# Cross-attention scores of a two-block decoder: one float32 product becomes three terms of rounded and remaining parts

## The chip, the cores and the metric

One core of one Trainium2 chip runs the whole program in one launch. The metric is the device time of one execution in microseconds (us); the median of three runs of the kernel before is 2508.31 us (2506.42 to 2509.89). The engines are named as in the profile: PE (TensorE, matmuls; PEld is its weight load), DVE (VectorE), ACT (ScalarE), POOL (GpSimd) and SP (SyncE, which here only issues DMAs).

## What is computed

Two stacks of layers on 512 tokens of width 1024, in float32. The change lies in the cross-attention of the second block, which reads 256 memory tokens with 4 heads of width 256:

```python
def memory_cross_attention(x, mem, g_x, g_m, wq, wk, wv, wo):
    b, s, _ = x.shape
    h = rms_norm(x, g_x)
    m = rms_norm(mem, g_m)
    q = (h @ wq).reshape(b, s, XATTN_HEADS, XATTN_HEAD_DIM)
    k = (m @ wk).reshape(b, m.shape[1], XATTN_HEADS, XATTN_HEAD_DIM)
    v = (m @ wv).reshape(b, m.shape[1], XATTN_HEADS, XATTN_HEAD_DIM)
    sc = jnp.einsum("bshd,bmhd->bhsm", q, k).astype(jnp.float32) * (XATTN_HEAD_DIM ** -0.5)
    p = jax.nn.softmax(sc, axis=-1)
    o = jnp.einsum("bhsm,bmhd->bshd", p.astype(v.dtype), v).reshape(b, s, D_MODEL)
    return o @ wo
```

Everything else (retention layers, sparse attention, gated mixers, feed-forward parts, norms) is the same in both kernels.

## The kernel before

**Tiling.** Activations lie feature by feature in SBUF: a tile of 512 tokens (`T`) for each of the 8 blocks (`KB`) of 128 features. A product with a weight matrix is cut into units; unit `f` makes 128 output features for all tokens and ends in the bank `unit_ps[f % 2]`. It is 24 matmuls of 128x512: 8 blocks of the inner dimension times three terms, since nearly every product is made of float32r operands, a rounded part (`wh`, `ah`, `ch`) and what remains of the value (`wl`, `al`, `cl`): `wh*xh + wh*xl + wl*xh`.

**Who does what for a unit's weights.** SP loads 512 KB into `raw[u % 2]` once POOL is done with the unit two before it. ACT rounds it into `wh` (one instruction of 128x1024, in `ahead2(XQ + f)`: it waits for the end of unit `f` and for the landing of the weights of unit `f + 4`). POOL makes `wl = raw - wh` in two instructions of 128x512 and counts `w_lo` (L472).

**The stretch of the query projection, units XQ to XQ+7.** It follows the output projection of the mixers (`OUT`) and a norm: DVE sums the squares, PE averages them (`ssq`), ACT takes the root (L530) and DVE the reciprocal `rstd` (L1286). Each engine has its own hand-written order:

- PE: unit 0, `ssq`, unit 1, unit 2, `x_scores(0)`, unit 3, `x_turns(0)` (transposes of the weights of head 0), unit 4, `x_values(0)`, `x_scores(1)`, unit 5, `x_turns(1)`, unit 6, `x_values(1)`, `x_scores(2)`, unit 7, `x_turns(2)`, `x_scores(3)`, then the first units of the output projection `XO` with the rest of heads 2 and 3 between them. Head `h` reads the query units `2h` and `2h + 1`. A unit waits for its bank: unit `f` for the eviction of unit `f - 2`.
- DVE, for `f` from 0 to 7: waits for unit `f`, evicts it (`mult`, `xq_t[f] = unit_ps * rstd`, L1276 in the profile, line 1707 in the loop), and then, for `f` of 0 and 1, makes the remaining part `vl` of the memory's values (L1711); for odd `f` from 3 the remaining part of the transposed weights (L1696); for even `f` from 2 the softmax of head `(f - 2) / 2` (L1684 maximum, L1686, L1689 and a product on L1276), ahead of it from 4 on the remaining part of a head's result (L1703).
- ACT: the root, two copies of 128x1024 that round the memory's values (`vh`, L835), and then for each `f` the weights of unit `f + 4` (L495), for odd `f` the rounded transposed weights (L850), for even `f` the rounded result (L855) and the exponentials (L842).

`x_scores(h)` multiplies float32 operands directly, for 4 blocks of 128 tokens and 2 blocks of the head's width: the queries `xq_t` (in `d1`) are the stationary operand, the memory keys `mem_k` (in `b_f32`) the moving one of 256 columns:

```python
for c in range(NC):
    for b in range(2):
        last = pe.matmul(aux[:, 2 * (h % 2) + c // 2, (c % 2) * MEM:(c % 2 + 1) * MEM], xq_t[2 * h + b][:, c * P:(c + 1) * P],
                         mem_k[:, (2 * h + b) * MEM:(2 * h + b + 1) * MEM], start=(b == 0), stop=(b == 1))
last.then_inc(xs_mm, 1)
```

`go()` makes a DVE instruction wait for the one before it, and `did(...)` counts it. In the profile `xq_t` and the softmax's `x_p` both read as `d`, `vh` and `vl` as `bl`, `xth` and `xtl` as `bh`, and `mem_k` and `mem_v` as `b_f`.

Of the kernel before, what the change touches and what calls it, by code (L numbers as in the profile page):

```python
# [27 lines left out]
F32 = mybir.dt.float32  # L28
F32R = mybir.dt.float32r
I32 = mybir.dt.int32  # L30
BF16 = mybir.dt.bfloat16
ALU = mybir.AluOpType
ACT = mybir.ActivationFunctionType
AX = mybir.AxisListType.X

P = 128
T = 512
D = 1024
KB = D // P
# [27 lines left out]
MEM = 256  # L67
# [20 lines left out]
XQ = OUT + KB  # L88
# [45 lines left out]
def layer_stack_kernel(nc, d, out):  # L134

    ctx = ExitStack()
    with ctx:
        def sb(name, shape, dt=F32):
            return ctx.enter_context(nc.sbuf_tensor(name, shape, dt))

        def sem(name):
            return ctx.enter_context(nc.semaphore(name))
# [12 lines left out]
        bh, bl = sb("bh", [P, KB * T], F32R), sb("bl", [P, KB * T], F32R)  # L155
        with nc.sbuf_tensor("c_f32", [P, 2 * KB * T], F32) as c_f32:
            cf = c_f32
        ch, cl = sb("ch", [P, KB * T], F32R), sb("cl", [P, KB * T], F32R)
        d1, d2 = sb("d1", [P, KB * T]), sb("d2", [P, KB * T])

        with (nc.sbuf_tensor("decay_t", [P, HEADS * T], F32) as decay_t, nc.sbuf_tensor("cos_t", [P, T], F32) as cos_t,
# [20 lines left out]
        rstd = sb("rstd", [P, T])  # L182
        tmp = [sb(f"tmp{i}", [P, T]) for i in range(2)]
# [59 lines left out]
        mem_k = bf[:, 4 * T:8 * T]  # L243
        mem_v = bf[:, 12 * T:16 * T].rearrange("p (c v) -> p c v", c=2)
# [5 lines left out]
        p_first = d1[:, 2 * T:6 * T].rearrange("p (r k) -> p r k", r=REP)  # L250
        part_x = [d1[:, (4 + i) * T:(5 + i) * T] for i in range(2)]
        ffn_t = [d1[:, i * T:(i + 1) * T] for i in range(4)]
        xq_t = [d1[:, f * T:(f + 1) * T] for f in range(KB)]
        vh, vl = (bl[:, at:at + 4 * T].rearrange("p (c v) -> p c v", c=2) for at in (0, 4 * T))
        x_p = d2[:, 2 * T:4 * T].rearrange("p (c m) -> p c m", c=NC)
        xth, xtl = (bh[:, at:at + 2 * T].rearrange("p (m q) -> p m q", m=2) for at in (0, 2 * T))
# [1 line left out]
        unit_ps = [ctx.enter_context(nc.psum_tensor(f"unit_ps{i}", [P, T], F32)) for i in range(2)]  # L258
        aux = ctx.enter_context(nc.psum_tensor("aux", [P, 4, T], F32))
# [25 lines left out]
        w_hi, w_lo, mm, evac = sem("w_hi"), sem("w_lo"), sem("mm"), sem("evac")  # L285
# [27 lines left out]
        src2 = sem("src2")  # L313
        mean_out = sem("mean_out")
        w_att, p_act = sem("w_att"), sem("p_act")
        v_hi, v_lo, xt_lo = sem("v_hi"), sem("v_lo"), sem("xt_lo")
        xs_mm, xs_shift, x_exp, xp_ready, xt_mm, xt_copy, xo_mm = (sem(n) for n in (
            "xs_mm", "xs_shift", "x_exp", "xp_ready", "xt_mm", "xt_copy", "xo_mm"))
# [7 lines left out]
        def half_blk(t, k, half):  # L326

            return t[:, k * T + half * T // 2:k * T + (half + 1) * T // 2]
# [157 lines left out]
        def _(act):  # L486
# [5 lines left out]
            def split_w(u, j):  # L492

                act.wait_ge(raw_in[j % 2], 16 * 1 + (u - j % 2) * 8)
                act.activation(wh[j][:], raw[j % 2][:], ACT.Copy).then_inc(w_hi, 1)  # L495
# [32 lines left out]
            def sqrt_ms(n, dst=rstd[:], src=stat_ps, bias=eps[:, 0:1]):  # L528
                act.wait_ge(ssq_mm, n)
                act.activation(dst, src, ACT.Sqrt, bias=bias).then_inc(std_done, 1)  # L530
# [114 lines left out]
            def ahead2(u):  # L645

                act.wait_ge(mm, u + 1)
                if u + 4 < U_END:
                    split_w(u + 4, u % 4)
# [37 lines left out]
            for i in range(2):  # L687
                for g in range(2):
                    out_g = 1 - g if i else g
                    lanes = slice(out_g * HD, out_g * HD + HD)  # L690
# [141 lines left out]
            norm_units2(OUT, 2, ch, sq_out)  # L832
            sqrt_ms(LAYERS * 2 + 3)
            for m in range(2):
                act.activation(vh[:, m], mem_v[:, m], ACT.Copy).then_inc(v_hi, 1)  # L835


            def x_exps(h):
                act.wait_ge(xs_shift, h + 1)
                s_x = aux[:, 2 * (h % 2):2 * (h % 2) + 2].rearrange("p b (c m) -> p (b c) m", m=MEM)  # L840
                for c in range(NC):
                    act.activation(x_p[:, c], s_x[:, c], ACT.Exp, scale=DV ** -0.5,  # L842
                                   bias=row[:, 0, c:c + 1], accum_out=row[:, 1, c:c + 1]).then_inc(x_exp, 1)

            def x_turned(h):
                for m in range(2):
                    act.wait_ge(xt_mm, 2 * h + m + 1)
                    if h:
                        act.wait_ge(xo_mm, 2 * h)
                    act.activation(xth[:, m], o_ps[m], ACT.Copy).then_inc(xt_copy, 1)  # L850

            def x_hi(h):
                for b in range(2):
                    act.wait_ge(xo_mm, 2 * h + b + 1)
                    act.activation(blk(ah, 2 * h + b), aux[:, 2 * (h % 2) + b], ACT.Copy).then_inc(in_hi, 1)  # L855

            for f in range(KB):
                ahead2(XQ + f)
                if f % 2:
                    if f >= 3:  # L860
                        x_turned((f - 3) // 2)
                elif f >= 2:
                    if f >= 4:
                        x_hi((f - 4) // 2)
                    x_exps((f - 2) // 2)
# [59 lines left out]
        def _(dve):  # L925
# [337 lines left out]
            last = [(dve_step, step[0])]  # L1263

            def go():

                dve.wait_ge(*last[0])

            def did(ins, s=dve_step):
                count[id(s)] = count.get(id(s), 0) + 1  # L1270
                ins.then_inc(s, 1)
                last[0] = (s, count[id(s)])

            def mult(dst, a, b, s=dve_step):
                go()
                did(dve.tensor_tensor(dst, a, b, ALU.mult), s)  # L1276
# [115 lines left out]
            for k in range(KB):  # L1392
                dve.wait_ge(mem_hi, k // 2 * 2 + 2)
                lanes = slice(k * MEM, (k + 1) * MEM)
# [297 lines left out]
            def x_turned_lo(h):  # L1692
                for m in range(2):
                    dve.wait_ge(xt_copy, 2 * h + m + 1)
                    go()
                    did(dve.tensor_tensor(xtl[:, m], o_ps[m], xth[:, m].bitcast(F32), ALU.subtract), xt_lo)  # L1696

            def x_lo(h):
                for b in range(2):
                    k = 2 * h + b  # L1700
                    dve.wait_ge(in_hi, IL + k + 1)
                    go()
                    did(dve.tensor_tensor(blk(al, k), aux[:, 2 * (h % 2) + b], blk(ah, k).bitcast(F32), ALU.subtract), in_lo)  # L1703

            for f in range(KB):
                dve.wait_ge(mm, XQ + f + 1)
                mult(xq_t[f], unit_ps[(XQ + f) % 2][:], rstd[:], evac)
                if f < 2:
                    dve.wait_ge(v_hi, f + 1)
                    go()  # L1710
                    did(dve.tensor_tensor(vl[:, f], mem_v[:, f], vh[:, f].bitcast(F32), ALU.subtract), v_lo)  # L1711
                elif f % 2:
                    x_turned_lo((f - 3) // 2)
                else:
                    if f >= 4:
                        x_lo((f - 4) // 2)
                    x_softmax((f - 2) // 2)
# [107 lines left out]
        def _(pe):  # L1825
# [192 lines left out]
            for n in range(CMP_BLOCK):  # L2018
                for i in range(2):
                    for g in range(2):  # L2020
                        lanes = slice(g * HD, g * HD + HD)
                        out_g = 1 - g if i else g
                        last = pe.matmul(aux[out_g * HD:out_g * HD + HD, 2 * i + g, 0:N_CMP], cmp_w1[i][lanes, n], cmp_win[i][lanes, n],
                                         start=(n == 0), stop=(n == CMP_BLOCK - 1))
# [4 lines left out]
            for g in range(2):  # L2029
                lanes = slice(g * HD, g * HD + HD)  # L2030
                pe.matmul(o_ps[0][lanes, 0:N_CMP], cmp_w2[0][lanes], cmp_hid[0][lanes], start=True, stop=True).then_inc(cmp_mm, 1)
            for g in range(2):
                lanes = slice((1 - g) * HD, (1 - g) * HD + HD)
# [4 lines left out]
            for c in range(NC):  # L2038
                for i in range(2):
                    last = pe.transpose(aux[:, c // 2, (c % 2) * DV + i * P:(c % 2) * DV + (i + 1) * P], y_gm[i][:, c * P:(c + 1) * P], ident[:])  # L2040
# [21 lines left out]
            for k in range(KB):  # L2062
                for c in range(2):
                    col = (k % 2) * MEM + c * P
                    last = pe.transpose(aux[:, k // 2, col:col + P], mem_raw[:, c, k * P:(k + 1) * P], ident[:])
# [115 lines left out]
            for i in range(2):  # L2181
                for c in range(NC):
                    for half in range(2):
                        g = 2 * i + half
                        last = pe.matmul(o_ps[i][half * HD:half * HD + HD, c * P:(c + 1) * P], v_ln[:, c, g * HD:(g + 1) * HD], gm_wt[:, g * P:(g + 1) * P],
                                         start=True, stop=True)
# [57 lines left out]
            for at in range(4, KB):  # L2244
                pe.wait_ge(in_lo, IL + at + 1)
                for f in range(2):
                    last = out_part(f, PART_ORDER[at], at)
                    if at == KB - 1:
                        last.then_inc(mm, 1)
            for f in range(2, 4):  # L2250
                for at in range(4, KB):
                    last = out_part(f, PART_ORDER[at], at)
# [3 lines left out]
            IL += 2 * KB  # L2256

            def x_scores(h):
                pe.wait_ge(evac, XQ + 2 * h + 1 + 3)
                if h >= 2:  # L2260
                    pe.wait_ge(in_lo, IL + 2 * (h - 2) + 2)
                for c in range(NC):
                    for b in range(2):
                        last = pe.matmul(aux[:, 2 * (h % 2) + c // 2, (c % 2) * MEM:(c % 2 + 1) * MEM], xq_t[2 * h + b][:, c * P:(c + 1) * P],  # L2264
                                         mem_k[:, (2 * h + b) * MEM:(2 * h + b + 1) * MEM], start=(b == 0), stop=(b == 1))
                last.then_inc(xs_mm, 1)

            def x_turns(h):
# [49 lines left out]
            for k in (6, 7):  # L2318
                pe.wait_ge(in_lo, IL + k + 1)
                for f in range(2):  # L2320
                    last = xo_part(f, (k,))
# [21 lines left out]
            for n, (u, f, half) in enumerate(LAST_PARTS):  # L2343
# [3 lines left out]
                for k in range(n_k):  # L2347
                    for q, (w, v) in enumerate(((wh, ah), (wh, al), (wl, ah))):
                        last = pe.matmul(unit_ps[u % 2][:, 0:T // 2], w[(DNG[2] + f) % 4][:, k], half_blk(v, k, half),  # L2349
                                         start=(k == 0 and q == 0), stop=(k == n_k - 1 and q == 2))  # L2350
# [91 lines left out]
```

## Time and profile before

| | |
|---|---|
| median of 3 runs | 2508.31 us (2506.42 to 2509.89) |
| the profiled execution, its own time | 2508.62 us |
| its span, first to last instruction | 2506.8 us |
| PE busy | 2488.3 us, 99% |
| PEld, DVE, ACT, POOL busy | 82%, 49%, 37%, 50% |
| the chain that ended last: PE, DVE, ACT | 95%, 4%, 1% |
| the score matmuls (L2264) | 64 records, 14.6 us busy |
| granted clock of PE | 0.997 of full speed (2.4 GHz) |

A span is what the trace covers; the 1.8 us between it and the execution's own time lie around it. A float32 matmul leaves two records, so the 64 records of L2264 are 32 matmuls. Where one engine is busy throughout, what counts is what it executes and where it stands still; idle time of the others costs nothing until PE waits for them.

### The profile page before, as it was taken

To read this page: it belongs to the slowest core of one execution; us is meant where nothing else is said; L and a number is where in the kernel's file an instruction comes from. 1 tells how busy PE (TensorE), PEld (TensorE's weight loads), DVE (VectorE), ACT (ScalarE), POOL (GpSimd) and SP (SyncE) were. 2 spreads that over 40 slices of the span, in tenths; PEclk is the share of its full clock that TensorE was granted. 3 is DMA by queue.
4 is the path that set the end of the run, shared out by engine and by line. 5 is a ranking of instruction groups with operands and counts; after the bars stand their busy time and mean duration, and the time that the engine had idled before them with its cause. 6 is when DMAs were issued, how large, how long until landed. Compare 5 with 4: busy or idle time off the path is not lost.

```text
span 2506.8 us, 34796 instructions
## 1 busy us (share of the span) xinstructions
PE 2488.3 (99%) x11934; PEld 2050.8 (82%) x11934; DVE 1226.6 (49%) x1436; ACT 917.4 (37%) x1322; POOL 1257.5 (50%) x879
## 2 busy tenths in 40 slices
PE   9999999999999999999999999999999999999998
PEld 8888888888888888888888888888877888888887
DVE  7444612453322542555135423227887755788364
ACT  5223423332222332334234322223457644444233
POOL 6555355655545554544455545555523443555454
PEclk9999999999999999999999999999999999999999
DMA  5332233333333333322333333337321232333332
GB/s 166 101 92 85 67 100 93 101 93 101 92 101 93 101 93 99 94 76 76 99 94 101 93 99 95 97 96 161 87 59 60 76 93 68 92 99 94 100 91 78
DMA packets 441982, 235.38 MB, mean 94 GB/s; under 512 B 16145, under 2 KB 436113, under 8 KB 441873
## 3 DMA queue, kind: packets, MB, share of 16 engines
q1 hardware_dynamic: 441440, 233.26, 32.4%
q8 instruction: 67, 1.10, 0.2%
q10 hardware_dynamic: 432, 0.67, 0.1%
q14 instruction: 43, 0.34, 0.0%
HBM read 231.81 MB, written 2.10 MB: 93 GB/s over the span
## 4 chain that ended last, share of the span: by engine, by line
PE 95%; DVE 4%; ACT 1%; issue 0%; DMA 0%; DVEq 0%; ACTq 0%
PE unit_ps L1847 62%; PE unit_ps L1992 13%; PE unit_ps L1978 7%; PE aux L1884 2%; PE unit_ps L1884 1%; PE o_banks L1884 1%; DVE c_f L1313 1%; PE aux L2220 1%; PE aux L2114 1%; PE unit_ps L2082 1%; PE unit_ps L2154 1%; PE o_banks L1925 1%; PE aux L2264 1%; PE aux L2052 0%; PE aux L2285 0%; PE unit_ps L2349 0%
## 5 line engine op out<-in xcount | busy, mean ns | idle before, releaser
L472 POOL TENSOR_TENSOR wl<-raw,wh 128x512 fp32r<-128x512 f32 x862 | 1251.1, 1472 | 1229.2 <-ACT wh L543 819.6
L543 ACT ACTIVATE wh<-raw 128x1024 fp32r<-128x1024 f32 x304 | 322.6, 1061 | 1023.7 <-PE unit_ps L1847 965.9
L1847 PE MATMUL unit_ps<-ah,wh 128*128 128x512 f32 x1280 | 503.1, 393 | 0.0
L1847 PE MATMUL unit_ps<-ah,wl 128*128 128x512 f32 x1280 | 498.6, 390 | 0.0
L1847 PE MATMUL unit_ps<-al,wh 128*128 128x512 f32 x1280 | 498.6, 390 | 0.0
L1847 PE MATMUL unit_ps<-bh,wh 128*128 128x512 f32 x768 | 300.1, 391 | 0.0
L1847 PE MATMUL unit_ps<-bh,wl 128*128 128x512 f32 x768 | 299.1, 389 | 0.0
L1847 PE MATMUL unit_ps<-bl,wh 128*128 128x512 f32 x768 | 299.1, 389 | 0.0
L1847 PEld LDWEIGHTS unit_ps<-al,wh 128*128 128x128 f32 x1280 | 240.3, 188 | 51.5 <-issue 1.9
L1847 PEld LDWEIGHTS unit_ps<-ah,wh 128*128 128x128 f32 x1280 | 240.3, 188 | 51.0 <-issue 1.9
L1847 PEld LDWEIGHTS unit_ps<-ah,wl 128*128 128x128 f32 x1280 | 240.3, 188 | 50.0
L495 ACT ACTIVATE wh<-raw 128x1024 fp32r<-128x1024 f32 x111 | 117.8, 1061 | 184.7 <-PE unit_ps L1992 111.9
L1847 PEld LDWEIGHTS unit_ps<-bh,wh 128*128 128x128 f32 x768 | 144.2, 188 | 30.8 <-issue 1.0
L1847 PEld LDWEIGHTS unit_ps<-bl,wh 128*128 128x128 f32 x768 | 144.1, 188 | 30.3 <-issue 0.5
L1847 PEld LDWEIGHTS unit_ps<-bh,wl 128*128 128x128 f32 x768 | 144.1, 188 | 30.0
L1244 DVE TENSOR_TENSOR x<-unit_ps,x 128x512 f32 x48 | 33.2, 692 | 213.5 <-PE unit_ps L1847 213.5
L1992 PE MATMUL unit_ps<-ch,wl 128*128 128x512 f32 x320 | 124.6, 389 | 0.0
L1992 PE MATMUL unit_ps<-ch,wh 128*128 128x512 f32 x320 | 124.6, 389 | 0.0
L1992 PE MATMUL unit_ps<-cl,wh 128*128 128x512 f32 x320 | 124.6, 389 | 0.0
L1234 DVE TENSOR_TENSOR tmp<-unit_ps,rstd 128x512 f32<-128x512 f32 x64 | 44.2, 691 | 134.8 <-PE unit_ps L1847 134.0
L1743 DVE SCALAR_TENSOR_TENSOR d<-tmp,vectors,d 128x511 f32<-128x511 f32 x88 | 106.0, 1205 | 1.5
L1847 PE MATMUL unit_ps<-ch,wh 128*128 128x512 f32 x256 | 99.7, 389 | 0.0
(403 smaller groups left out, 3873.3 us busy)
## 6 DMA issues: line engine op xcount, KB each, us to landing
raw<-w_in_dram SPq DMA_DIRECT2D x144, 512.0 KB, 4.0
raw<-w_up_dram SPq DMA_DIRECT2D x64, 512.0 KB, 4.0
raw<-w_down_dram SPq DMA_DIRECT2D x64, 512.0 KB, 4.1
raw<-up_dram SPq DMA_DIRECT2D x44, 512.0 KB, 3.8
raw<-w_conv_out_dram SPq DMA_DIRECT2D x16, 512.0 KB, 4.1
raw<-w_ret_out_dram SPq DMA_DIRECT2D x16, 512.0 KB, 4.1
raw<-w_o_dram SPq DMA_DIRECT2D x16, 512.0 KB, 4.1
raw<-down_dram SPq DMA_DIRECT2D x16, 512.0 KB, 3.9
```

The costliest lines, as they stand in the source:

```text
L472: last = pool.tensor_tensor(wl[j][:, half], raw[j % 2][:, half], wh[j][:, half].bitcast(F32), ALU.subtract)
L495: act.activation(wh[j][:], raw[j % 2][:], ACT.Copy).then_inc(w_hi, 1)
L543: act.activation(wh[j][:], raw[j % 2][:], ACT.Copy).then_inc(w_hi, 1)
L1234: dve.tensor_tensor(tmp[0][:], unit_ps[j % 2][:], rstd[:], ALU.mult).then_inc(evac, 1)
L1244: dve.tensor_tensor(blk(x, f), unit_ps[j % 2][:], blk(x, f), ALU.add).then_inc(evac, 1)
L1313: did(dve.scalar_tensor_tensor(out=cv_a[i], in0=src, scalar=w, in1=cv_a[i], op0=ALU.mult, op1=ALU.add))
L1743: did(dve.scalar_tensor_tensor(out=into, in0=tmp[n % 2][:, 0:T - s_], scalar=ffn_taps[:, w_, b:b + 1], in1=into, op0=ALU.mult, op1=ALU.add ...
L1847: last = pe.matmul(unit_ps[j % 2][:], w[j][:, k], v[:, k * T:(k + 1) * T], start=(k == 0 and n == 0), stop=(k == KB - 1 and n == 2))
L1884: last = pe.matmul(v_ps[group][c], v[:, col:col + P], two_k(w[j])[:, k], start=(k0 + k == 0 and w is wh and v is ah), stop=(k0 + k == KB - ...
L1925: last = pe.matmul(o_ps[b][:, n * P:(n + 1) * P], v_tok[:, n, col:col + P], p_dec[h % 2][:, n * P:(n + 1) * P], start=True, stop=(n == 0))
L1978: last = pe.matmul(dst, w[u % 4][:, k], v[:, k * n:(k + 1) * n], start=(k == 0 and q == 0), stop=(k == n_k - 1 and q == 2))
L1992: last = pe.matmul(unit_ps[u % 2][:], w[u % 4][:, k], v[:, k * T:(k + 1) * T], start=(at == 0 and q == 0), stop=(at == n_k - 1 and q == 2))
```

## The change

The scores of a head are made as `qh*kh + ql*kh + qh*kl` in float32r. The keys are split once: ACT rounds them into `kh` with two copies of 128x1024, which stand ahead of the two copies of the values, and DVE writes the remaining part `kl` over `mem_k`. A query unit no longer goes from its bank to `xq_t`: DVE evicts it to `tmp[f % 2]`, ACT rounds it into `xqh`, DVE subtracts into `xql`, and only then the unit's query is ready. `x_scores(h)` waits for `q_lo` instead of `evac`. In the profile of the new kernel `kh`, `xqh` and `xql` read as `d_f32r` and `kl` as `bh`.

```diff
+        xqh, xql = ([dr[:, at + f * T:at + (f + 1) * T] for f in range(4)] for at in (0, 12 * T))
+        kh, kl = dr[:, 4 * T:8 * T], bh[:, 4 * T:8 * T]
...
             sqrt_ms(LAYERS * 2 + 3)
             for m in range(2):
+                lanes = slice(m * D, (m + 1) * D)
+                act.activation(kh[:, lanes], mem_k[:, lanes], ACT.Copy).then_inc(k_hi, 1)
+            for m in range(2):
                 act.activation(vh[:, m], mem_v[:, m], ACT.Copy).then_inc(v_hi, 1)
...
             for f in range(KB):
                 ahead2(XQ + f)
+                act.wait_ge(evac, XQ + f + 3)
+                act.activation(xqh[f % 4], tmp[f % 2][:], ACT.Copy).then_inc(q_hi, 1)
...
             for f in range(KB):
                 dve.wait_ge(mm, XQ + f + 1)
-                mult(xq_t[f], unit_ps[(XQ + f) % 2][:], rstd[:], evac)
-                if f < 2:
-                    dve.wait_ge(v_hi, f + 1)
-                    go()
-                    did(dve.tensor_tensor(vl[:, f], mem_v[:, f], vh[:, f].bitcast(F32), ALU.subtract), v_lo)
+                mult(tmp[f % 2][:], unit_ps[(XQ + f) % 2][:], rstd[:], evac)
+                if f == 0:
+                    for m in range(2):
+                        lanes = slice(m * D, (m + 1) * D)
+                        dve.wait_ge(k_hi, m + 1)
+                        go()
+                        did(dve.tensor_tensor(kl[:, lanes], mem_k[:, lanes], kh[:, lanes].bitcast(F32), ALU.subtract), k_lo)
+                dve.wait_ge(q_hi, f + 1)
+                go()
+                did(dve.tensor_tensor(xql[f % 4], tmp[f % 2][:], xqh[f % 4].bitcast(F32), ALU.subtract), q_lo)
+                if f == 1:
+                    for m in range(2):
+                        dve.wait_ge(v_hi, m + 1)
+                        go()
+                        did(dve.tensor_tensor(vl[:, m], mem_v[:, m], vh[:, m].bitcast(F32), ALU.subtract), v_lo)
+                elif f == 0:
+                    pass
                 elif f % 2:
                     x_turned_lo((f - 3) // 2)
...
             def x_scores(h):
-                pe.wait_ge(evac, XQ + 2 * h + 1 + 3)
+                pe.wait_ge(q_lo, 2 * h + 2)
+                if h == 0:
+                    pe.wait_ge(k_lo, 2)
...
                     for b in range(2):
-                        last = pe.matmul(aux[:, 2 * (h % 2) + c // 2, (c % 2) * MEM:(c % 2 + 1) * MEM], xq_t[2 * h + b][:, c * P:(c + 1) * P],
-                                         mem_k[:, (2 * h + b) * MEM:(2 * h + b + 1) * MEM], start=(b == 0), stop=(b == 1))
+                        k = 2 * h + b
+                        lanes = slice(k * MEM, (k + 1) * MEM)
+                        for n, (q, kk) in enumerate(((xqh, kh), (xql, kh), (xqh, kl))):
+                            last = pe.matmul(aux[:, 2 * (h % 2) + c // 2, (c % 2) * MEM:(c % 2 + 1) * MEM], q[k % 4][:, c * P:(c + 1) * P], kk[:, lanes],
+                                             start=(b + n == 0), stop=(b == 1 and n == 2))
```

**How the orders move.** On DVE, from the reciprocal of the norm to the end of the softmax of head 0, the kernel before has:

```order
RECIPROCAL rstd<-rstd 128x512
TENSOR_TENSOR d<-unit_ps,rstd 128x512
TENSOR_TENSOR bl<-b_f,bl 128x1024
TENSOR_TENSOR d<-unit_ps,rstd 128x512
TENSOR_TENSOR bl<-b_f,bl 128x1024
TENSOR_TENSOR d<-unit_ps,rstd 128x512
TENSOR_REDUCE row<-aux 128x4
TENSOR_SCALAR row<-row 128x4
RECIPROCAL row<-row 128x4
TENSOR_TENSOR d<-d,row 128x1024
```

and the changed one, at the same place:

```order
RECIPROCAL rstd<-rstd 128x512
TENSOR_TENSOR tmp<-unit_ps,rstd 128x512
TENSOR_TENSOR bh<-b_f,d_f32r 128x1024 x2
TENSOR_TENSOR d_f32r<-tmp,d_f32r 128x512
TENSOR_TENSOR tmp<-unit_ps,rstd 128x512
TENSOR_TENSOR d_f32r<-tmp,d_f32r 128x512
TENSOR_TENSOR bl<-b_f,bl 128x1024 x2
TENSOR_TENSOR tmp<-unit_ps,rstd 128x512
TENSOR_TENSOR d_f32r<-tmp,d_f32r 128x512
TENSOR_REDUCE row<-aux 128x4
TENSOR_SCALAR row<-row 128x4
RECIPROCAL row<-row 128x4
```

The two subtractions of the keys stand ahead of the query of unit 0, both subtractions of the values now stand between the queries of units 1 and 2, and each eviction is followed by a subtraction of its own.

On ACT, from the root of the norm to the exponentials of head 0, before:

```order
ACTIVATE rstd<-aux,eps 128x512
ACTIVATE bl<-b_f 128x1024 x2
ACTIVATE wh<-raw 128x1024 x3
ACT_TABLE_LOAD
ACTIVATE d,row<-aux,row 128x256 x4
```

and changed:

```order
ACTIVATE rstd<-aux,eps 128x512
ACTIVATE d_f32r<-b_f 128x1024 x2
ACTIVATE bl<-b_f 128x1024 x2
ACTIVATE wh<-raw 128x1024
ACTIVATE d_f32r<-tmp 128x512
ACTIVATE wh<-raw 128x1024
ACTIVATE d_f32r<-tmp 128x512
ACTIVATE wh<-raw 128x1024
ACTIVATE d_f32r<-tmp 128x512
ACT_TABLE_LOAD
ACTIVATE d,row<-aux,row 128x256 x4
```

The rounding of a weight (`wh<-raw`) and that of a query (`d_f32r<-tmp`) now take turns, and the first weight stands behind two copies more.

## Rows read from the trace of the kernel before

**Rows 1.** The page: busy time and share of each engine.

```profile
PE 2488.3 (99%) x11934; PEld 2050.8 (82%) x11934; DVE 1226.6 (49%) x1436; ACT 917.4 (37%) x1322; POOL 1257.5 (50%) x879
```

**Rows 2.** The chain that ended last, in the query projection: start us, us, what.

```profile
2033.90 3.45 PE aux L2264 x16
2037.36 5.46 PE unit_ps L1978 x24
2042.82 0.87 PE o_banks L2274 x8
...
2078.77 0.87 PE o_banks L2274 x8
2079.64 3.63 PE aux L2264 x16
2083.27 2.75 PE unit_ps L2303 x12
2086.02 2.73 PE aux L2285 x12
```

**Rows 3.** The same view, near the end of the program.

```profile
2479.92 8.29 PE unit_ps L2349 x69
```

**Rows 4.** The timeline of DVE: start us, us, what, [idle before <-releaser].

```profile
2027.23 0.69 DVE L1276 TENSOR_TENSOR d<-unit_ps,rstd 128x512 f32<-128x512 f32 x1
2027.83 1.22 DVE L1711 TENSOR_TENSOR bl<-b_f,bl 128x1024 fp32r<-128x1024 f32 x1
2029.15 0.69 DVE L1276 TENSOR_TENSOR d<-unit_ps,rstd 128x512 f32<-128x512 f32 x1
2029.76 1.53 DVE L1711 TENSOR_TENSOR bl<-b_f,bl 128x1024 fp32r<-128x1024 f32 x1
...
2037.39 1.23 DVE L1684 TENSOR_REDUCE row<-aux 128x4 f32<-128x1024 f32 x1 [2.76 <-PE aux L2264]
...
2041.04 1.22 DVE L1276 TENSOR_TENSOR d<-d,row 128x1024 f32<-128x1024 f32 x1
```

**Rows 5.** The timeline of DVE, of units of OUT, then of POOL in single instructions.

```profile
2012.75 0.69 DVE L1667 TENSOR_TENSOR d<-d 128x512 f32<-128x512 f32 x1
...
2017.70 1.61 DVE L1667 TENSOR_TENSOR d<-d 128x512 f32<-128x512 f32 x1
...
2018.71 1.74 POOL L472 TENSOR_TENSOR wl<-raw,wh 128x512 fp32r<-128x512 f32 x1
...
2027.87 2.34 POOL L472 TENSOR_TENSOR wl<-raw,wh 128x512 fp32r<-128x512 f32 x1
...
2030.25 2.19 POOL L472 TENSOR_TENSOR wl<-raw,wh 128x512 fp32r<-128x512 f32 x1
```

**Rows 6.** The timeline of ACT.

```profile
2023.60 2.00 ACT L835 ACTIVATE bl<-b_f 128x1024 fp32r<-128x1024 f32 x2
2025.50 1.05 ACT L495 ACTIVATE wh<-raw 128x1024 fp32r<-128x1024 f32 x1
2028.50 1.06 ACT L495 ACTIVATE wh<-raw 128x1024 fp32r<-128x1024 f32 x1 [1.95 <-PE unit_ps L1978]
2034.18 1.06 ACT L495 ACTIVATE wh<-raw 128x1024 fp32r<-128x1024 f32 x1 [4.62 <-DMA raw<-wq_dram]
...
2050.54 0.60 ACT L855 ACTIVATE ah<-aux 128x512 fp32r<-128x512 f32 x1 [0.30 <-PE aux L2285]
```

**Rows 7.** Instructions that touch the tile raw, 2020 to 2050: the way from issue to landing.

```profile
DMA to landing us min/median/max: 3.7/3.8/3.9
```

**Rows 8.** The timelines behind the end of unit 7: ACT, DVE, POOL.

```profile
2078.80 1.06 ACT L495 ACTIVATE wh<-raw 128x1024 fp32r<-128x1024 f32 x1 [2.06 <-PE unit_ps L1978]
...
2078.80 0.69 DVE L1276 TENSOR_TENSOR d<-unit_ps,rstd 128x512 f32<-128x512 f32 x1 [0.59 <-PE unit_ps L1978]
2080.38 1.49 DVE L1696 TENSOR_TENSOR bh<-o_banks,bh 128x512 fp32r<-128x512 f32 x2 [0.88 <-ACT bh L850]
...
2079.94 2.50 POOL L472 TENSOR_TENSOR wl<-raw,wh 128x512 fp32r<-128x512 f32 x2 [9.10 <-ACT wh L495]
```

## Prediction of the time after the change

> **What bounds the kernel now.** I read the page's busy shares first: PE is busy 99% of the span [rows 1], every other engine half of it or less. So an edit counts by what it takes from PE's work and by the time for which it makes PE stand still. Then the chain that ended last, in the stretch of the query projection: it stays on PE without a gap, from the scores of head 0 through unit 3 to the transposes, and again from the transposes of head 2 through the scores of head 3 into the output projection [rows 2]. Nothing there is slack on PE; every wait that the change makes PE take is added in full. Last, the timelines of DVE, ACT and POOL beside it show how close each hand-over is.
>
> **Part 1: what PE executes.** The scores of a head are 16 records in 3.45 us [rows 2], 8 float32 matmuls of 431 ns. They become 8 x 3 = 24 float32r matmuls of 256 columns. The nearest rows of that form are the last units of the program, 69 matmuls in 8.29 us, 120 ns each [rows 3], with as many weight loads. 24 x 0.120 = 2.88 us, 0.57 less for a head, and for four heads **-2.3 us**. The bounds are narrow: a loss of weight-load cover would show in [rows 3] too, since each of those matmuls has its own load.
>
> The page "TensorE: Matmul & The Clock Gate" of the Trainium skill (Back-to-back issue gap) gives 262 cycles for 256 columns, 109 ns at 2.4 GHz. By it a head would be 2.6 us and the four would save 3.3 us instead of 2.3, and the sum below would be 1.0 us lower; the row says 120 ns, and I keep the row.
>
> **Part 2: what two SBUF operands cost on DVE.** The new subtractions read both operands from SBUF, and so must be priced beside POOL. Alone such an instruction is 0.69 us for 512 columns [rows 5] and 1.22 for 1024 [rows 4]. Beside POOL the two engines take turns. DVE's 1.22 us from 2027.83 to 2029.05 stretched the POOL instruction of 2027.87 to 2.34, that is to 2030.21, 1.16 us after DVE ended; DVE's next, begun at 2029.76, ended at 2031.29, 1.08 after that, and POOL's next at 2032.44, 1.15 after that [rows 4, 5]. DVE does get its turn between POOL's two halves: its instruction of 2017.70 ended at 2019.31, and POOL's second half (from 2018.71) only 1.14 later, at 2020.45 [rows 5]. An eviction, which reads a bank, kept its 0.69 us while POOL ran [rows 4]. So in contention: 512 columns 0.55 us once its turn has come, 1024 columns 1.08, a POOL half 1.15, and each waits for the other's current instruction.
>
> The Trainium skill has the rule ("SBUF — State Buffer", Who interferes with whom): a DVE instruction with two SBUF inputs and a GpSimd instruction that reads SBUF exclude each other for a whole instruction, one with a single SBUF input does not. The trace agrees. The old way out of the bank was of the harmless kind, the new `ql` is of the other; without the rule the sum below is 0.2, with it 4.4.
>
> **Part 3: the first head.** I carry the steps forward on the clock of this trace (us after 2000). Unchanged: the eviction of unit 0 starts at 27.23, unit 1 ends at 28.3, unit 2 at 33.7.
> - ACT copies the keys before the values. Two copies took 1.9 us from 23.60 to the weights at 25.50 [rows 6]; four end at 27.4. Weights 4: 27.4 to 28.45 (1.9 us later than now). Query 0 (an ACT copy of 512 columns, 0.60 [rows 6]): to 29.0. Weights 5: to 30.0.
> - DVE and POOL: `kl` first half 27.83 to 29.05; POOL 29.05 to 30.20; `kl` second half to 31.28; POOL's second half to 32.43; `ql` of unit 0 to 32.98; then POOL's first half of weights 5 to 34.13, beside it the eviction of unit 1 to 33.8 and ACT's rounding of it to 34.45. POOL's second half took its turn at 34.13, so `ql` of unit 1 waits for 35.4 and ends at 35.95. PE wants it at 33.75: **stall of 2.2 us** ahead of the scores of head 0. Scores to 38.9, unit 3 to 44.3.
> - DVE goes on with `vl` twice, 36.05 to 38.6, evicts unit 2 by 39.4 (a job that was done at 2034.6 before), ACT rounds it by 40.05. The weights of unit 6 were requested when POOL finished those of unit 4, 32.43, and land 3.8 us later [rows 7]; ACT rounds them at 36.4 to 37.5, and POOL's halves run after `vl` to 39.75 and 41.03. So `ql` of unit 2 ends at 41.6 and the softmax of head 0 begins at 41.7. It takes 4.87 us from its maximum to the end of its product (2037.39 to 2042.26, [rows 4]): 46.55. The transposes, which PE reached with 0.5 us in hand before (2042.26 against 2042.82), now wait from 44.3 to 46.6: **stall of 2.2 us**. The exponential table's load falls behind the rounding of query 2 and is hidden by the wait for the maximum.
>
> The two stalls hang together: what matters is that DVE's chain ends at 46.6, where PE without stalls would be at 33.74 + 2.88 + 5.46 = 42.1. Together **+4.5 us**. Without POOL in the way (0.69 and 1.22 each, turns not taken) the same chain gives `ql` of unit 1 at 33.3, no first stall, and an end of the softmax at 43.1: +1.0. That is the lower bound.
>
> **Part 4: heads 1 and 2.** Here I cost the change at nothing. Between the end of unit 4 or 6 and the end of the scores PE has `x_values` and the scores, 2.73 + 2.88 us; the query is rounded behind the weights 1.65 us after the unit's end and `ql` takes up to 1.35 more (both as in part 5), and the softmax begins with the scores' end as before. The cover is 2.6 us; if it were gone, each head would lose its excess at the transposes.
>
> **Part 5: the last head.** Between unit 7 and the scores of head 3 stand only transposes of 0.87 us [rows 2]. From unit 7's end (2078.78): eviction to 2079.49, weights on ACT 2078.80 to 2079.86 [rows 8], rounding of the query behind them from 2079.77 to about 2080.4. `ql` could start at 2080.43, where the remaining part of the transposed weights starts now [rows 8]. POOL has begun its first half at 2079.94 [rows 8] and holds until 2081.2; `ql` ends at 2081.8. PE is ready at 2079.65: **+2.15 us**; without POOL in the way `ql` ends at 2081.1, +1.45. The softmax of head 3 hides behind the same 5.5 us of PE work as now.
>
> **Sum.** -2.3 + 4.5 + 2.15 = **+4.4 us**. The profiled execution, 2508.62 us (span 2506.8 and 1.8 around it), becomes 2513.0; it stands 0.3 above the median of the three runs, so on the median's scale 2508.3 + 4.4 = 2512.7 us.
>
> **The rivals.**
> - *POOL is not in the way* (its halves and DVE's subtractions miss each other): -2.3 + 1.0 + 1.45 = +0.2, 2508.5 us. Against it: POOL's weights follow ACT's at once, and ACT's stand right ahead of each query. In between lies the case in which one `ql` of the first units slips ahead of a POOL half: +3.2, 2511.5 us.
> - *The stalls vanish and only the saving stays*: 2506.0 us. It would need `ql` of unit 7 within 0.87 us of the unit's end, against an eviction and a rounding of 0.69 + 0.6 alone.
> - *Clearly slower*: a POOL instruction that is already queued is let in ahead of a waiting DVE one, so that POOL keeps both halves together. The place is each `ql` behind weights just rounded: unit 7 (+1.2, a half), and units 0 and 2, whose ends set the chain of part 3 (+1.15 each). Two of the three give +6.7, 2515.0, all three 2516.2. It decides from the first of them on: +5.5 is past 0.2%. For it: a half begins the moment the other ends. Against it: the turns of [rows 5].
>
> **How the numbers follow.** 0.2% of this time, 5.0 us, is about what a measurement can tell from no change, so the line is at 2513.3. The forecast (both mechanisms as priced, 2511.8 to 2513.8) has 0.56, of which 0.09 lies over the line; POOL less in the way, 2508.5 to 2511.5, 0.20; clearly slower 0.21; the saving alone or better 0.03, of which 0.01 is under 2503.3. Faster 0.01, same 0.69, slower 0.30. The range takes the whole forecast, most of the case with less of POOL, and the slower case with two turns lost: 2509.0 to 2515.0.
>
> **What would show it.** The chain should show 24 records of the score line in 2.9 us for a head. PE should stand idle at three places: before the scores of head 0 and of head 3 with the `ql` line as releaser, and before the transposes of head 0 with the softmax's product, 2.2 us each. The subtraction lines should show 512 columns in 0.7 to 1.8 us and not 0.69 throughout. Heads 1 and 2 should show no wait. I am wrong in part 3 if POOL's rows of 2.3 us are missing, in part 1 if the 24 records take more than 3 us, and in part 4 if the transposes of head 1 or 2 wait.

## The result, and the profile after

The changed kernel takes 2513.63 us (median of 9 runs, 2512.51 to 2519.94) against 2508.78 us for the kernel before, 9 runs in the same comparison: a ratio of 1.0024, 95% interval 1.0016 to 1.0032. It is slower, by 4.9 us between the medians, or by 6.0 by the ratio. In a second comparison it was 2514.39 against 2507.48 us (1.0023, 1.0014 to 1.0032). The forecast was 2512.7 us in a range of 2509.0 to 2515.0.

The page of the profiled execution, which with 2519.94 us was the slowest of the nine, says little by itself. What answers to [rows 1]:

```profile
span 2518.2 us, 34891 instructions
...
PE 2493.8 (99%) x11966; PEld 2055.8 (82%) x11966; DVE 1242.1 (49%) x1446; ACT 923.5 (37%) x1332; POOL 1260.3 (50%) x879
```

PE shows more busy time than before although it was given less to do, which already points to its clock. The page's span is 11.4 us longer, more than twice what the medians differ by, so the two pages can't be subtracted. 5.4 of the 11.4 us had passed before the changed stretch began: over all the executions below the norm's reciprocal starts anywhere between 2021.9 and 2029.1 us, in code ahead of it that is mostly identical.

The table by stages shows where the 5.4 us come from (stage: length, busy time and count of PE and of PEld, DVE, ACT, POOL, granted clock of PE, DMA share and GB/s). First two stages of the kernel before, then the same of the changed kernel:

```profile
1775.00:1785.00 10.00, 9.25 (x100) 7.49 (x101) 9.04 (x11) 3.04 (x10) 2.34 (x2) 1.00 0.22 58
1840.00:1855.00 15.00, 15.00 (x124) 12.54 (x124) 12.98 (x18) 11.83 (x26) 2.51 (x2) 0.89 0.25 71
```
```profile
1775.00:1785.00 10.00, 8.51 (x78) 7.08 (x79) 6.78 (x8) 1.18 (x5) 1.09 (x1) 0.66 0.22 57
1840.00:1855.00 15.00, 15.00 (x121) 11.82 (x117) 11.57 (x14) 8.00 (x17) 4.29 (x4) 0.77 0.13 36
```

PE has two levels of clock, 2.4 GHz (1.00) and 1.2 GHz (0.50). By these averages it ran at the lower one for some 14 us of the 25 in this execution of the changed kernel and for some 3 in that of the kernel before. Half of the difference, some 5 us, is an estimate of what it lost by that, far ahead of anything that the change touches. In the stage from 1860 to 1875 both have 0.89. So I measure **the stretch**, from the start of that reciprocal to the first eviction of the output projection XO. In the timeline of DVE these are, for the kernel before:

```profile
2023.74 3.35 DVE L1286 RECIPROCAL rstd<-rstd 128x512 f32<-128x512 f32 x1 [1.94 <-ACT rstd L530]
...
2100.01 0.69 DVE L1639 TENSOR_TENSOR x<-unit_ps,x 128x512 f32 x1 [2.89 <-PE unit_ps L2303]
```

76.3 us. For the changed kernel, with the start of the reciprocal and what follows it up to the softmax of head 0:

```profile
2029.10 3.35 DVE L1295 RECIPROCAL rstd<-rstd 128x512 f32<-128x512 f32 x1 [1.94 <-ACT rstd L534]
...
2033.19 3.45 DVE L1722 TENSOR_TENSOR bh<-b_f,d_f32r 128x1024 fp32r<-128x1024 f32 x2
2036.75 1.60 DVE L1725 TENSOR_TENSOR d_f32r<-tmp,d_f32r 128x512 fp32r<-128x512 f32 x1
...
2039.84 1.42 DVE L1725 TENSOR_TENSOR d_f32r<-tmp,d_f32r 128x512 fp32r<-128x512 f32 x1 [0.70 <-ACT d_f32r L867]
2041.37 2.55 DVE L1730 TENSOR_TENSOR bl<-b_f,bl 128x1024 fp32r<-128x1024 f32 x2
...
2045.41 1.43 DVE L1725 TENSOR_TENSOR d_f32r<-tmp,d_f32r 128x512 fp32r<-128x512 f32 x1 [0.70 <-ACT d_f32r L867]
2046.95 1.22 DVE L1693 TENSOR_REDUCE row<-aux 128x4 f32<-128x1024 f32 x1
...
2050.59 1.22 DVE L1285 TENSOR_TENSOR d<-d,row 128x1024 f32<-128x1024 f32 x1
...
2111.32 0.69 DVE L1648 TENSOR_TENSOR x<-unit_ps,x 128x512 f32 x1 [2.89 <-PE unit_ps L2329]
```

82.2 us, 5.9 more. These lines answer to [rows 4]: `ql` (L1725) takes 1.4 to 1.6 us where its columns alone would take 0.69, and the softmax starts at 2046.95, which is 17.85 us after the reciprocal's start against 13.65 before. The chain that ended last (start us, us, what) shows what PE made of it:

```profile
2061.16 2.87 PE aux L2290 x24
2064.03 5.47 PE unit_ps L1999 x24
...
2088.54 1.35 DVE d_f32r L1725
2089.94 4.64 PE aux L2290 x24
2094.57 2.75 PE unit_ps L2329 x12
```

The 24 score matmuls (L2290) of head 1 take 2.87 us, those of head 3, behind the wait for `ql`, 4.64. The view of waits of PE in the same stretch (who waited <- for whom: us in total, times, longest):

```profile
PE aux L2290 <- DVE d_f32r L1725: 4.2, 2, 2.2
PE o_banks L2300 <- DVE d L1285: 0.4, 1, 0.4
```

And the table by stages:

```profile
2039.00:2041.30 2.30, 0.24 (x2) 0.00 (x0) 1.56 (x2) 0.63 (x1) 1.71 (x2) 1.00 0.80 228
2041.30:2046.00 4.70, 4.68 (x26) 4.59 (x27) 3.73 (x4) 2.29 (x3) 3.05 (x2) 0.64 0.40 112
...
2089.90:2094.50 4.60, 4.56 (x25) 4.57 (x26) 1.38 (x2) 0.00 (x0) 1.12 (x1) 0.63 0.41 114
```

The first of these stages holds the stand-still itself, the other two follow the two stand-stills of PE ahead of the scores: there the granted clock is 0.64 and 0.63 on average, so for the greater part of each PE has the lower of its two levels. That was not in the forecast.

### The profile page after: what moved, and what is told of

It is laid out like the page before. It is cut to its first block, busy times and chain, and to the rows that moved or that the text cites. A ratio compares the mean times of both kernels' runs of the same rounds, so it can differ in the third digit from the quotient of the medians.

```text
span 2518.2 us, 34891 instructions
## 1 busy us (share of the span) xinstructions
PE 2493.8 (99%) x11966; PEld 2055.8 (82%) x11966; DVE 1242.1 (49%) x1446; ACT 923.5 (37%) x1332; POOL 1260.3 (50%) x879
## 4 chain that ended last, share of the span: by engine, by line
PE 94%; DVE 4%; ACT 1%; issue 1%; DMA 0%; DVEq 0%; ACTq 0%
PE unit_ps L1868 62%; PE unit_ps L2013 13%; PE unit_ps L1999 6%; PE aux L1905 2%; PE unit_ps L1905 1%; PE o_banks L1905 1%; DVE c_f L1322 1%; PE aux L2241 1%; PE unit_ps L2103 1%; PE aux L2135 1%; PE unit_ps L2175 1%; PE o_banks L1946 1%; PE aux L2073 0%; PE aux L2311 0%; PE unit_ps L2375 0%
```

## The experiments

All times of the stretch are from the profiled execution of each run, all ratios from timed runs on the same chip as the kernel before.

**The form alone.** The kernel before with

```diff
-                        last = pe.matmul(aux[...], xq_t[2 * h + b][:, c * P:(c + 1) * P], mem_k[:, (2 * h + b) * MEM:(2 * h + b + 1) * MEM], start=(b == 0), stop=(b == 1))
+                        k = 2 * h + b
+                        for n, (q, kk) in enumerate(((ch, ch), (cl, ch), (ch, cl))):
+                            last = pe.matmul(aux[...], q[:, k * T + c * P:k * T + (c + 1) * P], kk[:, k * MEM:(k + 1) * MEM], start=(b + n == 0), stop=(b == 1 and n == 2))
```

> The matmul form alone: the kernel before, with the scores of a head as 24 float32r matmuls of 256 columns instead of 8 float32 ones, on the normed activations ch and cl, which lie ready (so the scores are those of other numbers); no split of queries or keys, the wait still on the eviction. The stretch from the start of the norm's reciprocal to the first eviction of the output projection is 76.3 us in the kernel before and 82.2 in the changed one. If the form saves what part 1 of the prediction says, a head is 2.9 us and the stretch 76.3 - 2.3 = 74.0, total 2.3 us under before. Rival, the form itself costs (its weight loads are not covered beside float32 transposes): stretch 76.3 or more.

The stretch runs from 2022.47 to 2096.47, 74.0 us; the median is 2504.92 us, ratio 0.9990 (0.9981 to 1.0000). The heads in the chain:

```profile
2032.64 2.87 PE aux L2266 x24
...
2076.68 3.05 PE aux L2266 x24
```

So the form saves 2.3 us, and the changed kernel loses some 8 us elsewhere in its first profiled execution.

**Is POOL in the way?** The changed kernel, where POOL subtracts 8 columns in place of 1024 for nine units, from XQ+4 to XO+4:

```diff
...
+                    pool.wait_ge(w_hi, u + 1)
+                    j = u % 4
+                    pool.tensor_tensor(wl[j][:, 0, 0:8], raw[j % 2][:, 0, 0:8], wh[j][:, 0, 0:8].bitcast(F32), ALU.subtract).then_inc(w_lo, 1)
...
```

> The changed kernel, in which POOL subtracts 8 columns instead of 1024 for the weights of units XQ+4 to XO+4 (their remaining parts are old data). Theory: POOL's two halves hold up DVE's subtractions of two SBUF operands; without them these take 0.69 and 1.22 us, the stall ahead of the scores of head 0 goes, the transposes of head 0 wait 1.0 us, head 3 waits 1.45 instead of 2.3: stretch 77 to 78.5. Rival, the order of the steps alone makes the stalls and POOL does not matter: 82.2, the subtractions still at 1.3 to 1.6 us.

```profile
2031.28 2.55 DVE L1738 TENSOR_TENSOR bh<-b_f,d_f32r 128x1024 fp32r<-128x1024 f32 x2
2033.92 0.69 DVE L1741 TENSOR_TENSOR d_f32r<-tmp,d_f32r 128x512 fp32r<-128x512 f32 x1
...
2036.11 0.69 DVE L1741 TENSOR_TENSOR d_f32r<-tmp,d_f32r 128x512 fp32r<-128x512 f32 x1 [0.70 <-ACT d_f32r L883]
```

These are lines of DVE's timeline, and the subtractions are back at 0.69 us (and 2.55 for the pair, as `vl` had). PE's waits:

```profile
PE aux L2306 <- DVE d_f32r L1741: 1.5, 1, 1.5
PE o_banks L2316 <- DVE d L1301: 1.0, 1, 1.0
```

No wait ahead of the scores of head 0, 1.0 us at its transposes, 1.5 at head 3; stretch 2027.18 to 2104.00, 76.8 us, ratio 1.0007 (0.9997 to 1.0016). POOL's halves make 3.9 us of the loss where the clock is whole at head 3 (80.7, below), and the extra steps by themselves 2.8 (76.8 - 74.0), little more than the 2.3 that the form saves. POOL also frees the buffers of the weights sooner in this run, but no load stands in the changed kernel's chain in this stretch, so that is not what it gains.

**Does the clock fall because PE stands still?** Nine matmuls of 512 columns without a use ahead of the wait of heads 0 and 3:

```diff
+                if h in (0, XH - 1):
+                    for n in range(9):
+                        pe.matmul(aux[:, 2 * (h % 2)], ch[:, 0:P], ch[:, 0:T], start=True, stop=True)
                 pe.wait_ge(q_lo, 2 * h + 2)
```

> The changed kernel, with 9 matmuls of 512 columns (2.0 us of work without a use, into a bank that the scores then overwrite) put on PE where it stands still ahead of the scores of heads 0 and 3. Theory: after a 2 us stand-still the clock is granted at half for some us, and the scores of head 3 take 4.5 us instead of 2.9. With the filler the clock stays whole: head 3's scores 2.9 us, stretch 82.2 - 1.6 = 80.6; at head 0 nothing is won, since there the chain of DVE decides and the wait moves to the transposes, 1.9 us or so. Rival: the scores behind a wait are slow by themselves (uncovered weight loads, other tiles): head 3's stay at 4.5 us and the stretch at 82.2.

At head 3 it came as expected (chain, then the stage):

```profile
2084.44 3.13 PE aux L2293 x24
```
```profile
2084.40:2087.50 3.10, 3.06 (x25) 3.06 (x26) 1.38 (x2) 0.00 (x0) 1.14 (x1) 1.00 0.15 40
```

But the stretch is 82.4 us (2021.91 to 2104.32), not 80.6, and the ratio 1.0029 (1.0018 to 1.0041). The wait at head 0 moved to the transposes, 2.0 us, as it had to, and now the slow clock followed that one:

```profile
2045.98 6.94 PE unit_ps L1999 x24
```
```profile
2044.70:2048.50 3.80, 3.75 (x15) 3.17 (x16) 2.82 (x3) 1.61 (x3) 2.38 (x2) 0.62 0.05 14
```

Unit 3 takes 6.94 us instead of 5.47. The filler is no cure, and by itself the run leaves open whether the slow clock at head 3 would have come without the filler.

**A stand-still alone.** The kernel before, with float32 scores and no split:

```diff
+            pe.wait_ge(xt_lo, 2 * (XH - 1))
             x_scores(XH - 1)
```

> The kernel before with nothing but a wait: the scores of head 3 wait for the remaining part of the transposed weights of head 2, which ends 2.2 us after the point at which PE would begin. It prices a stand-still of the changed kernel's length at its place, with float32 scores and without any split. If only the time of waiting counts: stretch 76.3 + 2.2 = 78.5. If the clock falls behind a stand-still whatever caused it: 80.0 to 80.2, with records of the scores at up to twice their 216 ns.

```profile
PE aux L2264 <- DVE bh L1696: 2.3, 1, 2.3
```
```profile
2082.20:2086.00 3.80, 3.73 (x17) 3.32 (x18) 0.02 (x1) 0.00 (x0) 0.58 (x1) 1.00 0.46 133
```

2.3 us of waiting, a whole clock behind it, a stretch of 78.6 us (2024.11 to 2102.74) and a ratio of 1.0010 (1.0000 to 1.0019). The wait alone costs its length, and the clock need not fall.

**The changed kernel twice more, as it is.**

> The changed kernel once more, as it is. In its first profiled execution, 6 us slower than its median, the clock fell to half behind two of the stand-stills; behind stand-stills of the same length in the runs e3_early, e5_qfirst, e6_early2 and e8_idle it stayed whole. If the slow clock comes with some executions only, this one may show a stretch of 80.8 us (76.3 - 2.3 + 2.1 + 2.2 + 2.3 and 0.2 for the transposes) with all scores at 2.9 us; if it belongs to this order of work, 82.2 again.

> The same, a second look: 80.8 us in the stretch where the clock stays whole, up to 82.4 where it falls.

The first gives 82.3 us (2024.72 to 2106.99), the second 80.7 (2023.58 to 2104.29). Their heads 3, in the table by stages:

```profile
2085.50:2090.00 4.50, 4.39 (x25) 4.39 (x26) 1.44 (x3) 0.00 (x0) 1.20 (x1) 0.66 0.39 114
```
```profile
2084.40:2087.50 3.10, 3.06 (x25) 3.06 (x26) 1.38 (x2) 0.00 (x0) 1.13 (x1) 1.00 0.17 46
```

Same program, same wait of 2.2 us, and the clock falls in one and not in the other: 1.6 us between the two stretches. Their chains have the scores of head 3 at 4.46 us and at 3.14:

```profile
2085.61 4.46 PE aux L2290 x24
```
```profile
2084.44 3.14 PE aux L2290 x24
```
At head 0 it is the other way round. In the first the clock stayed whole and PE waited 2.0 us at the transposes; in the second it fell behind the first wait and the transposes waited 0.5. There a slow clock costs nearly nothing, since the chain of DVE decides.

**The last query ahead of the weights.**

```diff
-                ahead2(XQ + f)
+                if f < KB - 1:
+                    ahead2(XQ + f)
                 act.wait_ge(evac, XQ + f + 3)
                 act.activation(xqh[f % 4], tmp[f % 2][:], ACT.Copy).then_inc(q_hi, 1)
+                if f == KB - 1:
+                    ahead2(XQ + f)
```

> The changed kernel, with ACT rounding the query of unit 7 ahead of the weights instead of behind them. Theory: the last query is then ready before POOL begins with those weights; head 3 waits 1.3 us instead of 2.3, and if it is the length of the stand-still that brings the slow clock, its scores go back from 4.5 to 2.9 us: stretch 82.2 - 1.0 - 1.6 = 79.6. If the clock falls after the shorter stand-still too: 81.2. Rival, POOL and the weights do not set this wait: 82.2.

```profile
2081.80 0.70 DVE d_f32r L1728
2082.55 3.14 PE aux L2293 x24
```

`ql` takes 0.70 us, since it comes before POOL has anything to do, and head 3 waits 1.3 us. Stretch 79.9 us (2022.54 to 2102.43), ratio 1.0012 (1.0003 to 1.0022). The clock stayed whole in this execution even behind two waits of 2.0 us at head 0, so it doesn't tell whether a shorter wait is what kept it.

**The splits of keys and values ahead.** Four ACT copies in front of the mixers' output projection, and four DVE subtractions in its loop:

```diff
...
+                if f in (4, 5):
...
+                    did(dve.tensor_tensor(kl[:, lanes], mem_k[:, lanes], kh[:, lanes].bitcast(F32), ALU.subtract), k_lo)
+                elif f in (6, 7):
...
+                    did(dve.tensor_tensor(vl[:, m], mem_v[:, m], vh[:, m].bitcast(F32), ALU.subtract), v_lo)
```

> The changed kernel with the splits of keys and values moved ahead, into the output projection of the mixers (four ACT copies ahead of its weights, the four DVE subtractions between its units 3 and 7). Theory: the stalls at head 0 come from the chain of DVE that begins with them; without them eviction, rounding and subtraction of units 0 to 2 are done in time, both stalls and the slow clock behind them go: 82.2 - 4.5 = 77.7, of it 2.3 of waiting and 1.6 of slow clock left at head 3. Rival: the query's own three steps are too long there as well, the stall stays at 1 us or more and the stretch above 79.

The stretch is 77.5 us (2028.58 to 2106.06) and head 0 doesn't wait any more. Yet the median is 2514.89 us, no better than the changed kernel. Ahead of the stretch:

```profile
PE unit_ps L1999 <- DVE cl L1673: 3.7, 1, 3.7
```

The last subtraction of the values stood ahead of the last normed block on DVE, and unit 0 of the query waited 3.7 us for that block. Behind this wait the clock fell too, and part of that lies in the stretch:

```profile
2026.50:2031.50 5.00, 5.00 (x14) 3.46 (x15) 2.92 (x1) 1.63 (x2) 1.93 (x2) 0.66 0.35 94
```
```profile
2027.82 12.15 PE unit_ps L1999 x48
```

These 48 matmuls take 10.92 us at a whole clock (the splits in gaps, below), and since head 0 doesn't wait here, the 1.2 us are in the 77.5. That the stretch met the 77.7 expected is in part luck: the slow clock that was expected behind the wait of head 3 didn't come (3.14 us for its scores), and another one came in its place.

**The same, in gaps.** Only the keys ahead (after units 3 and 4 on DVE, two ACT copies); the values' two subtractions inside the softmax of head 0, where DVE waits for the exponentials, and behind the transposed weights of head 0:

```diff
...
+                if h == 0:
+                    v_rest(0)
                 dve.wait_ge(x_exp, NC * (h + 1))
...
```

> The changed kernel with only the keys' rounding ahead of the mixers' output projection, their subtractions between its units 3 and 5, and the two subtractions of the values in gaps of DVE (while it waits for the exponentials of head 0, and after the transposed weights of head 0). The run with all splits early won 4.7 us in the stretch and lost 3.4 to 5 us ahead of it, where the values' subtractions held up the last normed blocks. Theory: with DVE's gaps used both are had: the wait for the normed blocks ahead of the norm's factor stays at 0.3 us, the stretch is 76.3 - 2.3 + 2.2 = 76.2 if the clock stays whole behind head 3's wait, 77.8 if it falls. Rival: any work that DVE takes on ahead delays the norm; then the wait for the normed blocks is 1 us or more.

Stretch 76.3 us (2025.46 to 2101.74), median 2510.84, ratio 1.0004 (0.9995 to 1.0014). One wait of size is left in the stretch, and ahead of it 0.7 us twice, for a normed block and for the sum of squares, where 0.3 was expected:

```profile
PE aux L2295 <- DVE d_f32r L1733: 2.2, 1, 2.2
PE aux L1855 <- DVE d L1677: 0.7, 1, 0.7
PE unit_ps L2004 <- DVE cl L1673: 0.7, 1, 0.7
```

The clock is whole behind the wait of head 3 (scores 3.13 us), and the 48 matmuls of the query's first units take 10.92 us.

**And the last head covered.** With the last query ahead of the weights as above, and PE's tail as

```diff
-            x_scores(XH - 1)
             pe.wait_ge(in_lo, IL + 4)
             pe.wait_ge(w_lo, XO + 3)
-            xo_part(0, range(4))
+            pe.wait_ge(evac, XO + 1)
+            xo_part(0, range(3))
+            x_scores(XH - 1)
             x_values(XH - 2)
-            x_turns(XH - 1)
             pe.wait_ge(w_lo, XO + 4)
-            xo_part(1, range(4))
-            x_values(XH - 1)
+            xo_part(0, (3,))
+            xo_part(1, range(3))
+            x_turns(XH - 1)
+            xo_part(1, (3,))
             pe.wait_ge(in_lo, IL + 6)
             xo_part(0, (4, 5))
+            x_values(XH - 1)
             xo_part(1, (4, 5))
```

> The one before, with the query of unit 7 rounded ahead of the weights and 9 matmuls of the output projection put ahead of the scores of head 3, the others spread behind. If waits and the slow clock behind them are all that the change lost, no wait above 0.7 us is left and the stretch is 74.0 to 74.7, 1.6 to 2.3 us under the kernel before (total about 2506.5). Rival: the cover for the last softmax or for the last head's results is too short now and 2 us or more come back at another wait: stretch 76 or more.

> The run e7_both again, on these shared runs of the kernel before, for a narrower interval: stretch 73.8 us as then, median 2 us or so under before (ratio 0.999).

The stretch is 73.8 and 73.9 us (2023.62 to 2097.46, 2025.42 to 2099.34), 2.4 under the kernel before, and head 3 follows nine matmuls of XO without a wait:

```profile
2077.82 2.06 PE unit_ps L2337 x9
2079.88 2.87 PE aux L2298 x24
```

The medians are 2506.39 and 2507.17 us, ratios 0.9991 (0.9982 to 1.0000) and 0.9995 (0.9986 to 1.0004): some 7 us under the changed kernel, and against the kernel before a gain in the stretch that the whole time, which scatters by 5 us, doesn't show clear of no difference. Part of it goes ahead of the stretch, where PE waits 1.7 us for a normed block and the sum of squares in the one execution and 0.5 in the other; the keys' subtractions on DVE are the likely reason, but that wasn't tried apart.

## Why the prediction was right, and what it missed

**Right in direction, size and range; the missing term is the clock.** The forecast was +4.4 us; the stretch of the second repeat, with the clock whole at head 3, is 80.7 - 76.3 = +4.4. The other two executions, with the clock at half there, show +5.9 and +6.0. The timed runs say +4.9 and +6.9 by the medians of the two comparisons, +6.0 and +5.8 by their ratios, nearer to the upper value. A slow clock in part of the executions would put the time above 2512.7 like that, but three profiled executions don't show how often it comes, and slow clocks ahead of the stretch move the whole time too. The ratio lies past the line of 0.2%, to which I had given 0.30 in all; its interval, 1.0016 to 1.0032, includes the line.

**Part 1 held.** 24 matmuls in 2.87 us against 2.88 forecast, and the form alone is worth 76.3 - 74.0 = 2.3 us. The 262 cycles, 109 ns, of the Trainium skill ("TensorE: Matmul & The Clock Gate", Back-to-back issue gap) were not reached here; the rows at 120 ns were the better price.

**Part 2 held, and is shown.** The eight `ql` take 1.15 to 1.60 us beside POOL, and 0.69 with POOL out of the way. The rule of the Trainium skill named there ("SBUF — State Buffer", Who interferes with whom) agrees with these numbers, and what it is about decided this change: 80.7 us with POOL's work and 76.8 without.

**Part 3 held to 0.2 us, with its two waits.** Set to the same start of the reciprocal (5.36 us later in the profile after), the last `ql` before the scores of head 0 ends at 2035.9 (forecast 2035.95), `ql` of unit 2 at 2041.5 (2041.6), the softmax of head 0 at 2046.45 (2046.55). The first wait was 2.1 us for 2.2, the second 2.0 in the run with a whole clock for 2.2. Two small errors cancel in the +4.5: I let the scores of head 0 begin at 2033.74, where the chain has them at 2033.90 [rows 2], so PE without stalls would be at 42.2 and not 42.1, and the term would be 46.55 - 42.24 = 4.3; and I had not counted the 0.2 us by which the transposes take longer behind a wait (1.09 for 0.87). That the sum comes to +4.4 to the tenth is luck to that extent. That it is the end of DVE's chain that counts is borne out by the filler run and by the two repeats: whatever happens to PE before it, the end of the softmax stands.

**Part 4 held.** Heads 1 and 2 show no wait in any of the runs.

**Part 5 held in its wait, 2.2 us for 2.15, and failed in what follows it.** I took the scores behind the wait at 2.9 us. With the clock whole they took 3.14. Where it fell they took 4.46 and 4.64, and in the first of these two the first matmuls of XO 2.92 for 2.75: 1.5 us in either. No rival had this mechanism.

**The rivals.** POOL not in the way gives a stretch of 76.8 us, +0.5, where I had priced +0.2; 0.2 of the difference are the slower transposes again. POOL holding both halves together did not occur: each `ql` got its turn between two halves, in all runs.

**Shown and not shown.** Shown: the saving of the form, POOL's part, the place and length of the waits, and that a slow clock stands behind some of them. That the slow clock is caused by the stand-still is likely (it stands right behind one each time in this stretch) but not shown: of the waits of 2.2 to 2.3 us at head 3, two had it behind them and four not (the second repeat, the early splits, the splits in gaps, the stand-still alone). And a stand-still is not the only thing that comes before it. The kernel before has it in the middle of work, in the stage from 1840, behind 64 matmuls of 31 columns (chain, then the stage):

```profile
1838.14 3.69 PE o_banks L2122 x64
1841.84 4.55 PE unit_ps L2082 x24
```
```profile
1840.00:1846.00 6.00, 6.00 (x57) 5.96 (x56) 5.58 (x7) 4.00 (x10) 0.00 (x0) 0.72 0.31 90
```

PE is busy there throughout, and 24 matmuls of 256 columns take 4.55 us instead of 2.87. At this place too it comes in some executions, 8 of the 13 profiled ones, and not in the others. What decides stays open.

## What to carry to other kernels

When one engine is busy 99% of the time, a cheaper form of its instructions is worth only what the new steps that feed it leave: here -2.3 us of matmuls bought three steps on two engines, DVE and ACT, between a bank and its use, and cost +6.7 us (80.7 - 74.0) in waits and in slower work behind them. Write the chain of the feeding engines forward in absolute times, with the engine that takes turns with them in it (here POOL), and look for the step that comes right behind a unit's end; that gave both waits to 0.2 us. Splits of data that is known long before belong in gaps in which the engine waits for another, and not merely earlier: the four subtractions moved ahead brought the stretch from 80.7 to 77.5 us, but a wait of 3.7 us and a slow clock ahead of it when one stood in front of the norm's last block, and the median was no better.

## What was not expected of the hardware

- Behind stand-stills of 2.0 to 2.3 us the granted clock of PE fell to half in some executions and stayed whole in others, in one and the same program (0.66 and 1.00 in the stage behind the wait of head 3). It costs 1.5 us where PE decides and nearly nothing where PE then waits for another engine anyway. It also fell behind 64 matmuls of 31 columns without a stand-still (0.72 from 1840 to 1846 in the kernel before).
- With work without a use on PE in place of the waits ahead of the scores the clock was whole there, but the slow clock followed the next wait of 2.0 us (0.62 on average over the next 3.8 us). One execution doesn't show that the work is what kept it.
- DVE and POOL, both with two SBUF operands, take turns instruction by instruction even when POOL's two instructions follow each other at once: no `ql` took more than 1.60 us, which is its own 0.55 once its turn has come and less than one half of POOL's 1.15 more.
